# A hybrid encoder block on one core: part of the first expert table streamed and multiplied on TensorE instead of gathered

## The reference

```python
scores = einsum('thcd,hcnd->thcn', q, keys)         # 256 tokens, 8 heads, 2 halves, 128 keys
s_top, i_top = top_k(scores, 16)                    # then the 16 best of the 16 x 16 sums per head
idx  = 128 * i_top[first] + i_top[second]           # 128 experts of 16384 for each token
gate = softmax(best)
hid  = gelu(einsum('td,thkd->thk', x, U[idx]))      # U: 16384 x 2048, the first expert table
out  = einsum('thk,thkd->td', gate * hid, V[idx])   # V: 16384 x 2048, the second
```

## Time and profile before

| | |
|---|---|
| time, median of 3 runs | 2047.74 us (2046.32 to 2051.26) |
| span of the profiled execution | 2047.2 us |
| busy share | PE 70%, DVE 79%, ACT 42%, POOL 49% |
| moved by DMA | 601.8 MB, of which 268.4 MB are rows of the first table |
| weights and scores | 0 to 884 us |
| first table | 884 to 1515 us |
| tile 1's scatter | 1515 to 1564 us |
| second table and end | 1564 to 2047.2 us |

### The profile page before, as it was taken

One profiled execution on the slowest core, in us unless ns is written; L12 is line 12 of the kernel. 1 busy time (PEld: TensorE's weight loads), 2 busy tenths in 40 slices (PEclk: granted clock), 3 DMA queues, 4 the chain that ended last, 5 costly groups with the idle time before them and its releaser, 6 DMA issues.

```text
span 2047.2 us, 22565 instructions
## 1 busy us (share of the span) xinstructions
PE 1436.2 (70%) x7933; PEld 1248.8 (61%) x7933; DVE 1608.7 (79%) x1995; ACT 868.3 (42%) x1130; POOL 994.3 (49%) x699
## 2 busy tenths in 40 slices
PE   6999999999999999920000002212359999999997
PEld 6987998877888789920000001111247888888886
DVE  5465775454755556789999999977889999999998
ACT  4353443344343444311211226567856444444444
POOL 1002320000000000178888888888888788888862
PEclk9999999999999999965555555555569999999999
DMA  5555434444555555789999999999965999999996
GB/s 207 185 185 185 157 132 144 142 156 155 195 184 185 187 184 176 277 346 407 418 417 415 419 400 421 414 422 414 421 244 195 389 386 390 398 406 390 390 384 235
DMA packets 151803, 601.81 MB, mean 294 GB/s; under 512 B 14720, under 2 KB 14736, under 8 KB 118288
## 3 DMA queue, kind: packets, MB, share of 16 engines
q0 software_dynamic: 58048, 364.41, 44.0%
q1 hardware_dynamic: 93648, 236.02, 32.2%
HBM read 598.29 MB, written 2.10 MB: 293 GB/s over the span
## 4 chain that ended last, share of the span: by engine, by line
PE 55%; DVE 16%; issue 14%; POOL 7%; DMA 6%; ACT 2%; DVEq 0%; POOLq 0%; SPq 0%; ACTq 0%
PE acc L1715 7%; PE acc L1716 7%; PE acc L1717 7%; DVE slots L1470 6%; POOL slots L537 5%; PE acc L1698 4%; PE acc L1700 4%; PE acc L1701 4%; PE acc L2021 3%; PE scr L2022 3%; PE acc L2022 3%; DMA v_raw<-in_v_dense 3%; PE scr L2021 3%; PE scr L2023 3%; PE acc L2023 3%
## 5 line engine op out<-in xcount | busy, mean ns | idle before, releaser
L951 DVE TENSOR_TENSOR w_lo<-raw,w_hi 128x2048 fp32r<-128x2048 f32 x136 | 314.6, 2314 | 281.8 <-ACT w_hi L606 280.7
L1470 DVE SCALAR_TENSOR_TENSOR slots<-slots,acc 128x2048 f32<-128x2048 f32 x188 | 424.6, 2284 | 44.0 <-DMA slots<-in_peer_u,expert 41.7
L606 ACT ACTIVATE w_hi<-raw 128x2048 fp32r<-128x2048 f32 x136 | 260.1, 1913 | 409.0 <-PE acc L1717 263.3
L560 POOL DMA_INDIRECT starts<-in_v_gather,expert x256 | 365.1, 1426 | 92.9 <-DVE X L1620 77.7
L537 POOL DMA_INDIRECT slots<-in_peer_u,expert x256 | 250.2, 977 | 241.9 <-DVE expert L1442 145.2
L545 POOL TENSOR_TENSOR slots<-slots,N 128x2048 f32<-128x2048 f32 x62 | 280.5, 4524 | 37.2 <-DMA slots<-in_peer_u,expert 37.1
L887 ACT ACTIVATE v_hi<-v_raw 128x1344 fp32r<-128x1344 f32 x128 | 170.5, 1332 | 260.5 <-PE scr L2023 202.7
L800 ACT ACTIVATE slots<-slots 128x2048 f32<-128x2048 f32 x62 | 118.4, 1909 | 341.2 <-POOL slots L545 341.2
L1978 PE MATMUL scr<-hot_a,hot_b 128*128 128x128 f32 x448 | 92.4, 372 | 222.1 <-DVE hot_b L1515 158.4
L1620 DVE SCALAR_TENSOR_TENSOR X<-starts,weight,X 128x704 f32<-128x704 f32 x256 | 241.9, 945 | 0.7 <-DMA starts<-in_v_gather,expert 0.3
L1715 PE MATMUL acc<-w_hi,hT_hi 128*128 128x512 f32 x576 | 227.9, 396 | 2.5 <-DVE w_lo L951 2.5
(11 more groups left out here) (297 smaller groups left out, 3224.1 us busy)
## 6 DMA issues: line engine op xcount, KB each, us to landing
raw<-in_w_in SPq DMA_DIRECT2D x88, 1024.0 KB, 4.9
v_raw<-in_v_dense SPq DMA_DIRECT2D x128, 672.0 KB, 7.4
raw<-in_w_o SPq DMA_DIRECT2D x16, 1024.0 KB, 5.1
raw<-in_peer_wq SPq DMA_DIRECT2D x16, 1024.0 KB, 5.2
raw<-in_w_a_up SPq DMA_DIRECT2D x8, 1024.0 KB, 5.0
raw<-in_w_b_up SPq DMA_DIRECT2D x8, 1024.0 KB, 5.1
slots<-in_peer_u,expert POOLq DMA_INDIRECT x256, 9.6
starts<-in_v_gather,expert POOLq DMA_INDIRECT x256, 8.0
```

The source lines that it names most:

```text
L560: pool.indirect_dma_start(starts[j][:, :], None, v_gather[:, :], bass.IndirectOffsetOnAxis(ap=expert[:, s // NSEL, s % NSEL:s % NSEL + 1], ...
L606: a.activation(w_hi[:, m % 2, :, :], raw[:, m % 2, :, :], ACT.Copy).then_inc(hi_ready, 1)
L951: v.tensor_tensor(w_lo[:, m % 2, :, :], raw[:, m % 2, :, :], w_hi[:, m % 2, :, :].bitcast(fp32), ALU.subtract).then_inc(lo_ready, 1)
L1470: v.scalar_tensor_tensor(out=slots[j][:, :], in0=slots[j][:, :], scalar=1.0, in1=row, op0=ALU.mult, op1=ALU.mult, accum_out=hid_sum[:, t, ...
```

## The change

**Streaming.** U is laid out twice in DRAM: columns 768 to 2047 by rows (`u_gather`) and columns 0 to 767 as 128 blocks of 128 experts, 393 KB each (`u_dense`). SP streams the blocks through four buffers (`load_u`), and TensorE multiplies each with both token tiles, six fp32 matmuls of 256 columns; ScalarE copies two blocks at a time into `weight_all` (`evict`), which later holds the weight grid. The gathers bring 1280 columns (655 KB), and `dot`, `product` and `sum_product` work on 1280.

**Order.** Blocks 4i to 4i + 3 belong to group i + 1: ScalarE evicts two pairs of blocks and then takes the POOL row of the group, for groups 1 to 32. Twelve of the row buffers lie in the grids that the blocks fill, from the top down; the number of buffers in use falls from 13 (groups 1 to 14) by steps to 4 (groups 26 and 27), is 5 in groups 32 to 35 and 7 from group 36 on. In groups 25 to 28 VectorE takes all four rows. The gathers from q = 4 on wait for the last scores.

**Picks.** Groups 34 to 49 pick, four batches of four tokens each, the 128 dense products of each token out of its grid. Indices i, j (less 64) and their squares are stored to DRAM once per tile and read back as 5-row operands; a K = 5 matmul gives (index - n)^2; `hot_j` (ScalarE) makes the one-hot over j from it; `pick` (TensorE) adds four K = 5 matmuls (-2^100 off the place) and four fp32 matmuls of the one-hot with a column of the grid, read with a stride of 512 bytes; `find` (VectorE) takes the maximum.

**Scatter.** Both one-hots come from K = 5 squares: eight more fp32r matmuls per batch (`squares`), one Relu of 512 columns on ScalarE, one compare-and-multiply of 512 on VectorE. Tile 0's 32 batches lie in groups 50 to 63; of tile 1's copies one in three goes to VectorE. POOL makes no one-hots any more. X is kept in DRAM meanwhile (2 MB out, 2 MB back), since its place holds rows, tables and indices.

```diff
+ROW_AT = (32, 37, 42, 128, 133, 138, 48, 53, 58, 144, 149, 154, 107, 3, 8, 16, 21, 26, 192, 109)
+DVE_ALONE = range(100, 116)
+SELECT_FROM, SELECT_END = 34, 50
...
-                if q == 2 * FOUR:
+                if q == FOUR:
                     pool.wait_ge(unit_done, UNIT0[G_END])
+                    pool.wait_ge(scr_ready[1], use_number("score3"))
...
-                pool.indirect_dma_start(slots[j][:, :], None, u_rows,
+                pool.indirect_dma_start(slots[j][:, :], None, u_gather[:, :],
...
+            for m in range(BLOCKS):
+                n, u = m % len(UB_AT), m // 2
+                if m % 2 == 0 and u >= 2:
+                    pe.wait_ge(evicted, u - 1)
+                pe.wait_ge(u_landed[n], 16 * (m // len(UB_AT) + 1))
+                to = dense_bank[u % 2][:, (1 - m % 2) * S:(2 - m % 2) * S]
+                for k in range(UC):
+                    last = t_.matmul(to, ubs[n][:, k * P:(k + 1) * P], h2Tf[:, k, :], start=k == 0, stop=k == UC - 1)
+                last.then_inc(u_used, 1)
...
+            def pick(b):
+                room, g5 = row_group(b)
+                if b >= 2:
+                    pe.wait_ge(hid_found, b - 1)
+                t, n, to = b // BATCHES, b % BATCHES, picked[b % 2]
+                for c in range(SC):
+                    t_.matmul(to[:, c * P:(c + 1) * P], room[g5, c * P:(c + 1) * P], tests_i[g5, :], start=c == 0, stop=False,
+                              skip_group_check=True)
+                for c in range(SC):
+                    last = t_.matmul(to[:, c * P:(c + 1) * P], hot_a[:, b % 2, c, :], weight_all[t][:, :, n * SC + c],
+                                     start=False, stop=c == SC - 1, skip_group_check=True)
+                last.then_inc(picked_ready, 1)
...
             for i in range(GROUPS):
...
+                if 0 < i <= GROUPS // 2:
+                    evict(2 * i - 2)
+                    evict(2 * i - 1)
+                for b in selected(i):
+                    hot_j(b)
+                if i == SPREAD_FROM:
+                    hot_first(0)
+                for n in spread(i):
+                    hot_first(n + 1)
+                    scatter_out(n)
                 if on_pool(FOUR * i + FOUR - 1):
                     sum_product(FOUR * i + FOUR - 1)
...
                 for q in range(FOUR * i, FOUR * i + FOUR):
                     if q >= FOUR and not on_pool(q):
                         dot(q)
...
+                    for b in selected(i)[q % FOUR:q % FOUR + 1]:
+                        find(b)
...
+                if i == SELECT_FROM - 1:
+                    ones()
...
+            for w in range(BATCHES):
+                squares(w + 1)
+                scatter(w)
...
-                for c in range(SC):
-                    last = g.tensor_scalar(hot_a1[place(n)][:, c, :], iota_p, ijT[:, 1, 0, n * SC + c:n * SC + c + 1],
-                                           None, ALU.is_equal)
```

More of the change, by code:

```diff
@@ L60 @@
 STARTS_AHEAD = 4
-STARTS_BEFORE = 2
+STARTS_BEFORE = 1
 WIDE_FROM = 10 * CRING
@@ L136, in parts @@
[L136 to L157, removed]
+    return q % FOUR == FOUR - 1 and FOUR <= q < GATHERS - 1 and q not in DVE_ALONE
@@ new lines, in block_at, with overwritten, row_open, row_table @@
+def block_at(j):
+    return ROW_AT[j] - (G0_AT if ROW_AT[j] >= G0_AT else G1_AT)
+def overwritten(j):
+    if j >= HELD_ROW:
+        return None
+    return (P - 1 - (2 * block_at(j) + 9)) // 2
+def row_open(j, q):
+    if j < HELD_ROW:
+        return q < 2 * overwritten(j) - 4 and (q >= FOUR or j in FIRST_ROWS)
+    if j == HELD_ROW:
+        return FOUR <= q < P
+    return q >= (60 if j in SCORE_ROWS else 112 if j in ALL_ROWS else 144)
+def row_table():
+    last, table = [-GATHERS + j for j in range(len(ROW_AT))], []
+    for q in range(GATHERS):
+        j = min((j for j in range(len(ROW_AT)) if row_open(j, q)), key=lambda j: last[j])
+        last[j] = q
+        table.append(j)
+    return table
@@ new lines, with first_use, selected, spread @@
+ROW_OF = row_table()
+def buffer_of(q):
+    return ROW_OF[q]
+def uses_before(q, j):
+    return sum(SEM_OF[r] == SEM_OF[j] for r in ROW_OF[:q])
+def first_use(q):
+    return ROW_OF[q] not in ROW_OF[:q]
+def selected(i):
+    if not SELECT_FROM <= i < SELECT_END:
+        return range(0)
+    per = NT * BATCHES // (SELECT_END - SELECT_FROM)
+    return range(per * (i - SELECT_FROM), per * (i - SELECT_FROM + 1))
+def spread(i):
+    if i < SPREAD_FROM:
+        return range(0)
+    n = GROUPS - SPREAD_FROM
+    return range(BATCHES * (i - SPREAD_FROM) // n, BATCHES * (i - SPREAD_FROM + 1) // n)
@@ L160, in start_at, with parts, evictor, evictions @@
+def parts(i):
+    return range(min(56, 2 * i), min(56, 2 * i + 2))
+def evictor(w):
+    n = w - BATCHES
+    return "dve" if n >= 0 and (n % 3 == 2 or n == BATCHES - 1) else "act"
+def evictions(w, by):
+    return sum(evictor(v) == by for v in range(w))
 def start_at(s):
     return s % CRING if s < WIDE_FROM else (s - WIDE_FROM) % (2 * CRING)
+def start_count(s):
+    rows = sum(SEM_OF[r] == start_at(s) for r in ROW_OF)
+    return 16 * (rows + len(starts_before(s)) + 1)
 def weights_at(n):
@@ L1940, in score, with turn_norm @@
                 done(f"score{n}", last)
+            def turn_norm(n):
+                half = enter(f"dense{n}")
+                pe.wait_ge(h2_ready, NT)
+                for k in range(4 * n, min(UC, 4 * n + 4)):
+                    for t in range(NT):
+                        at0 = (k - 4 * n) * S + t * P
+                        last = t_.transpose(scr[:, half, at0:at0 + P], N1[:, t, k * P:(k + 1) * P], ident[:, :])
+                done(f"dense{n}", last)
             for n in range(4):
@@ new lines, in squares @@
+            def squares(w):
+                room, g5 = row_group(NT * BATCHES + w)
+                if w:
+                    pe.wait_ge(a_ready, w)
+                for c in range(SC):
+                    last = t_.matmul(square_a[:, c * P:(c + 1) * P], room[g5, c * P:(c + 1) * P], tests_i[g5, :],
+                                     start=True, stop=True)
+                last.then_inc(a_squared, 1)
+                if w:
+                    pe.wait_ge(b_hot_ready, w)
+                for c in range(SC):
+                    last = t_.matmul(square_b[:, c * P:(c + 1) * P], room[g5, c * P:(c + 1) * P], tests_j[g5, :],
+                                     start=True, stop=True)
+                last.then_inc(b_squared, 1)
@@ new lines, in scatter @@
+            def scatter(w):
+                t = w // BATCHES
+                before = w - 1 if w <= BATCHES else w - 2 if w > BATCHES + 1 else None
+                if w and before is not None:
+                    pe.wait_ge(scattered[evictor(before)], evictions(before + 1, evictor(before)))
+                pe.wait_ge(a_ready, w + 1)
+                pe.wait_ge(b_hot_ready, w + 1)
+                for c in range(SC):
+                    last = t_.matmul(scatter_bank[w % 2 if t else 0][:, c * P:(c + 1) * P], hot_b[:, w % 2, c, :],
+                                     hot_a[:, w % 2, c, :], start=True, stop=True)
```

511 lines of the change are left out of this document (303 added, 208 removed).

## The result

The changed kernel takes 2207.98 us, the median of 4 runs (2205.52 to 2211.53), beside 2047.45 for the kernel before: 1.0779 times as long, 95% interval 1.0762 to 1.0796. It is slower by 160 us where 9 us less were forecast, and lies above the range.

The account below looks back on a forecast made before the run. DMA bytes and POOL's program tied as bounds before TensorE, VectorE and DMA filled. Steps summed to 1555 at the second table against 1563.99, -9; 2047.2 - 9 + 0.5 gave about 2039 us, range 2014 to 2085.

Parts of the forecast that it names:

- head of group 34 at 1225: Streamed blocks: 128 at 2.65 us each, 339 us from 886, the gathers then standing at group 34.
- 12 for the start of the picks: After the blocks: 8 us until the first batch is through, 4 for groups 34 and 35; bounds 4 and 20.
- 8.42 a group: POOL in groups 34 to 63: 5.28 + 0.14 us for issues and gaps, 3.00 for the product; 29 groups, 244 us.
- 1555: Start of the second table: tile 1's scatter ending at 1551.5 us, then 3.5 as before; 1563.99 before the change.
- The step that failed: Picks and scatters: TensorE at full clock, 1.45 us a pick batch, 5.8 a group, so POOL paces; tile 1's scatter 1.7.
- in a ring: Tile 1's scatter: TensorE's 1.6 us, a Relu and a compare waiting on each other, 1.6 to 2.0 a batch, 1.7 taken.
- The rival: Picks: clock stays at 1.2 GHz, 3.2 us a batch, group 12.8, +70, 2109; shares 0.33 with doubled reads.
- The second step: Picks' matmuls reading the grid at a 512-byte stride: hidden, or up to 0.2 us more each; nothing taken.
- that rival's 9.5: Picks: strided reads at double cost make a group 9.5 us, +17, 2056; shares 0.33 with the half clock.
- The third: Hand-overs: tile 1's weights about 3.8 us behind the last dot, as before, plus one addition; its scatter 1.7 a batch.
- A term that was too high: POOL's four gather issues: 5.28 us of a group, with no room between them and the product.

Follow-up runs that it names:

- e4: The changed kernel with all tests by squares contracting 128 partitions instead of 5, through four masked copies of each test matrix; 2103.72 us.
- e11: e8 with ScalarE's sum of a POOL product put behind the next group's one-hots, for groups 33 to 49 alone; 2071.69 us, ratio 1.0095.
- e5: e4 with streamed products kept in lines of four experts per token (picks read 16-byte runs) and some row buffers given up to blocks earlier; 2092.96 us.
- e8: e5 with the first piece of rows loaded beside the last blocks and X's second half fetched back four batches later; 2082.85 us.
- e10: e4 unchanged, timed four more times; 2107.99 us, 1.0298 times the kernel before.
- e1: The changed kernel with all tests by squares contracting 32 partitions instead of 5; 2212.34 us, one run.

## Why the prediction was wrong

The stages can be cut at POOL's last 30 products, one for each group from 34 on, and at the second table's first matmul. After the change:

```profile
1240.34 2.90 POOL L682 TENSOR_TENSOR slots<-slots,N 128x1280 f32<-128x1280 f32 x1
...
1440.21 2.92 POOL L682 TENSOR_TENSOR slots<-slots,N 128x1280 f32<-128x1280 f32 x1
...
1575.11 2.92 POOL L682 TENSOR_TENSOR slots<-slots,N 128x1280 f32<-128x1280 f32 x1
...
1721.53 0.47 PE L2275 MATMUL acc<-v_hi,e_hi 128*128 128x512 f32 x1
```

The same cuts in e4 and in e11 beside the forecast's (head of group 34 at 1225 plus 5.42 of issues; 12 for the start of the picks and 8.42 a group; 1555), in us:

| stage | forecast | after | e4 | e11 |
|---|---|---|---|---|
| to group 34's product | 1230.4 | 1240.3 | 1238.7 | 1247.5 |
| groups 34 to 50 (picks) | 146.7 | 199.9 | 169.2 | 138.1 |
| groups 50 to 63 (scatter, tile 0) | 109.5 | 134.9 | 123.0 | 119.2 |
| to the second table | 68.4 | 146.4 | 86.2 | 86.4 |
| second table to the end of the span | 483.2 | 482.3 | 484.9 | 485.1 |

- **Right.** The blocks held the full clock; they took 2.71 us each, (1232.8 - 886) / 128, against 2.65. POOL's product of 1280 columns took 2.91 us (3.00 forecast), a dot 1.48 (1.43). The last stage was carried over unchanged, and is, within 2 us.
- **The step that failed** is the clock in the picks and both scatters: "TensorE, full clock, for a batch: ... 1.45, a group 5.8. So POOL sets the pace", and for tile 1 "1.6, in a ring ... I take 1.7". Measured 3.07 and 3.90. The rival stood in the prediction with its price, 3.2 us a batch and 2109; what dismissed it was "Against: at the half clock the batches follow each other without a gap, as from 1515 us, where the clock rose". That compared busy shares across different shapes: the rows it rests on the earlier trace rows have matmuls on 128 partitions only. The rival itself priced the picks alone (+70) and left the half clock out of the scatters, where it cost more: against e4, 31 us in the picks, 12 in tile 0's scatter, 60 in the tail.
- **The second step** is the strided read, "the read may hide, or cost up to as much again, 0.2 us per matmul; I take nothing". At the full clock, which the sum assumed, it costs (1.95 - 1.11) / 4 = 0.21 a matmul: the upper bound. e4's group of 9.66 us is that rival's 9.5. In the changed kernel itself the half clock hides it. By the Trainium skill, "Advanced Engine Details and Errata", section SBUF Cachelines, accesses that each go to another 16-byte line pay a penalty; e4 against e5 agrees (runs of 16 bytes: 1.11 us), the changed kernel's own 2.10 against 2.04 shows nothing of it.
- **The third** is a set of hand-overs priced too low or not at all. Tile 1's weights come 13 us behind the last dot after the change (1582.3 to 1595.5) and not 4: three one-hots of tile 0 stand ahead of them on VectorE (to 1588.8), and then VectorE waits 4.5 us for a ScalarE step that stands behind the copies of the same batches. A tail batch at the full clock is 1.83 us of gapless TensorE, not 1.7. A group with three scatter batches takes about 12 us in e4, one with two about 8. Even with clock and read mended, e11 is 18 us over the forecast in the last stage before the second table, 10 in tile 0's scatter and 17 at the start, 15 of which are later blocks (ending at 1239.7); only the picks beat it, by 9, for the next reason.
- **A term that was too high** hid part of this. Of the "5.28" that "go to four issues" 0.55 us are a wait for a gather, written in the product's row; so "there is no room between them" misread the row, and four issues take 4.73 us. In e11, where POOL runs some groups without a wait, they come every 7.8 us and not every 8.42:

```profile
1300.15 2.93 POOL L688 TENSOR_TENSOR slots<-slots,N 128x1280 f32<-128x1280 f32 x1
...
1307.96 2.92 POOL L688 TENSOR_TENSOR slots<-slots,N 128x1280 f32<-128x1280 f32 x1
```

Over 29 groups that is 18 us by which the forecast made this part too long; the misses above are that much larger than the difference in the time shows. e8's mean of 8.49 us (groups 36 to 44) is near 8.42 by chance: its groups take 7.8 and 9.1 in turn.

So of the 169 us between forecast and median, 100 are the clock together with the change of partitions (e10), and the rest is split as above: against the forecast e4 still loses 8 us to group 34, 22 in the picks (18 of them the strided read, by e5), 14 in tile 0's scatter and 18 behind it. No version tried at the full clock was faster than the kernel before: the forecast's 9 us were less than what the hand-overs cost. What stays open is whether a version with the blocks ending at 1225 and the tail's squares made elsewhere would beat the kernel before; none was tried.

## What to carry to other kernels

A stage that is to run "at the full clock" needs a row with its own shapes at that clock; a full TensorE on 5 to 64 partitions is not the same evidence as one on 128. If small contractions have to stand between full ones, widening them with zero rows costs nothing in columns, and here it gave back 100 us. And when the clock is mended, look again at every read that the slow clock had hidden.

## What the runs showed of the hardware

- With the same columns and result, tests on 5 or 32 partitions left the clock at 0.50 through some 470 us of nearly full TensorE (e1: 50.00 of 50.00 us at 0.50), but for a few us behind the residual; on 64 it was 0.50 too, but a clock raised by the residual held (1.00 from 1650 to 1700 us); on 128 it was 1.00 where TensorE was full (58.00 of 58.00 us). By the Trainium skill, "TensorE: Matmul & The Clock Gate", Part 1, activity releases the clock and idleness takes it back; these rows agree on the full-width matmuls and not on the others, behind which it fell in the middle of work without a gap.
- Matmuls on 5 partitions between those on 128 cost a batch 0.5 us at the half clock (3.90 against 3.41) and 0.3 at the full one (2.12 against 1.83), beyond their columns; on 64 it is 3.90 as well.
- Four fp32 matmuls that read one float every 512 bytes take 1.95 to 2.10 us at either clock; contiguous ones, or in runs of 16 bytes, go from 2.04 to 2.08 us at the half clock to 1.11 at the full one.
